# Query, key and value columns summed by feature quarters beside the first conditioning units

## The reference

```python
ada = jax.nn.silu(c) @ lp['w_ada'] + lp['b_ada']
sh1, sc1, g1, sh2, sc2, g2 = [a[:, None, :] for a in jnp.split(ada, 6, axis=-1)]
mix, states = mixer(x * (1 + sc1) + sh1, attend, conv_buf, h0, lp)
x = layer_norm(ALPHA * x + (1 + g1) * mix, lp['ln_g'][0], lp['ln_b'][0])
gt, up = jnp.split((x * (1 + sc2) + sh2) @ lp['w_ffn_in'], 2, axis=-1)
f = (jax.nn.silu(gt) * up) @ lp['w_ffn_out']
x = layer_norm(ALPHA * x + (1 + g2) * f, lp['ln_g'][1], lp['ln_b'][1])
...
proj = h @ lp['w_in'] + lp['b_in']
q, kvc, kvs, kvw, nsa_g, r_x, r_y, merge_g = jnp.split(proj, cuts, axis=-1)
```

## Time and profile before

| | |
|---|---|
| median of three runs | 1774.49 us |
| profiled execution | 1777.09 us, its span 1775.4 us |
| TensorE matmuls busy | 1737.5 us (98%) |
| TensorE weight loads busy | 1602.9 us (90%) |
| VectorE, ScalarE, GpSimd busy | 899.8, 711.3, 157.1 us |
| bytes moved by DMA | 384.05 MB, mean 216 GB/s |
| mean granted clock of TensorE | 0.99 |

### The profile page before, as it was taken

One profiled execution on the slowest core, in us unless ns is written; L12 is line 12 of the kernel. 1 busy time (PEld: TensorE's weight loads), 2 busy tenths in 40 slices (PEclk: granted clock), 3 DMA queues, 4 the chain that ended last, 5 costly groups with the idle time before them and its releaser, 6 DMA issues.

```text
span 1775.4 us, 34441 instructions
## 1 busy us (share of the span) xinstructions
PE 1737.5 (98%) x13514; PEld 1602.9 (90%) x13514; DVE 899.8 (51%) x1632; ACT 711.3 (40%) x1076; POOL 157.1 (9%) x271
## 2 busy tenths in 40 slices
PE   8989999999999999999999999999999999999997
PEld 3558879888999998889988899999999999999997
DVE  3233346655656655565873344444444444444565
ACT  2223227764545443343563333333333333333344
POOL 0001312213322311100000000000000000000001
PEclk9999999999999999999999999999999999999998
DMA  9998878766655647985647855545555454544552
GB/s 362 381 379 302 296 245 299 281 215 237 193 179 176 208 149 277 348 322 173 213 146 258 290 208 165 165 128 163 163 192 182 161 167 159 168 151 138 166 166 80
DMA packets 114151, 384.05 MB, mean 216 GB/s; under 512 B 14941, under 2 KB 15325, under 8 KB 113662
## 3 DMA queue, kind: packets, MB, share of 16 engines
q1 hardware_dynamic: 103248, 349.82, 57.1%
q0 software_dynamic: 10208, 32.32, 5.6%
q10 hardware_dynamic: 590, 0.44, 0.1%
HBM read 373.48 MB, written 9.03 MB: 215 GB/s over the span
## 4 chain that ended last, share of the span: by engine, by line
PE 90%; DMA 5%; DVE 2%; ACT 1%; SPq 1%; issue 1%; POOL 0%; POOLq 0%; ACTq 0%; DVEq 0%
PE bank L714 26%; PE bank L716 25%; PE bank L715 25%; DMA raw<-in_w_units 4%; PE bank L721 3%; PE bank L761 3%; PE bank L739 2%; PE bank L887 1%; SPq L478 1%; DVE wlo L377 1%; PE bank L1007 1%; PE bank L923 1%; DMA mgate<-mg 0%; ACT z L1510 0%; PE bank L954 0%
## 5 line engine op out<-in xcount | busy, mean ns | idle before, releaser
L714 PE MATMUL bank<-xhi,wlo 128*128 128x288 f32 x2544 | 759.2, 298 | 2.3 <-DVE wlo L377 1.7
L715 PE MATMUL bank<-xlo,whi 128*128 128x288 f32 x2544 | 751.0, 295 | 0.0
L716 PE MATMUL bank<-xhi,whi 128*128 128x288 f32 x2544 | 748.7, 294 | 0.0
L377 DVE TENSOR_TENSOR wlo<-raw,whi 128x1024 fp32r<-128x1024 f32 (+2 forms) x468 | 510.2, 1127 | 381.2 <-ACT whi L369 373.9
L369 ACT CAST whi<-raw 128x1024 fp32r<-128x1024 f32 (+2 forms) x468 | 434.6, 969 | 424.2 <-PE bank L716 273.8
L714 PEld LDWEIGHTS bank<-xhi,wlo 128*128 128x128 f32 x2544 | 477.5, 188 | 15.6 <-issue 13.7
L716 PEld LDWEIGHTS bank<-xhi,whi 128*128 128x128 f32 x2544 | 479.6, 189 | 0.0
L715 PEld LDWEIGHTS bank<-xlo,whi 128*128 128x128 f32 x2544 | 478.4, 188 | 0.6
L716 PE MATMUL bank<-hhi,whi 128*128 128x288 f32 x704 | 208.7, 296 | 0.0
L714 PE MATMUL bank<-hhi,wlo 128*128 128x288 f32 x704 | 208.3, 296 | 0.0
L715 PE MATMUL bank<-hlo,whi 128*128 128x288 f32 x704 | 205.2, 292 | 0.0
(11 more groups left out here) (332 smaller groups left out, 1674.9 us busy)
## 6 DMA issues: line engine op xcount, KB each, us to landing
raw<-in_w_units SPq DMA_DIRECT2D x556, 512.0 KB, 6.1
raw<-in_w_ffn_out_units SPq DMA_DIRECT2D x64, 384.0 KB, 3.1
raw<-in_w_ffn_out_units SPq DMA_DIRECT2D x64, 320.0 KB, 3.3
raw<-in_w_units SPq DMA_DIRECT2D x16, 448.0 KB, 8.6
mgate<-mg POOLq DMA_DIRECT2D x32, 144.0 KB, 4.3
mgl<-mgate POOLq DMA_DIRECT2D x16, 288.0 KB, 6.9
bz<-relrow POOLq DMA_DIRECT2D x16, 192.0 KB, 3.6
xt<-in_x SPq DMA_DIRECT2D x8, 288.0 KB, 7.4
```

The costliest lines, as they stand in the source:

```text
L377: nc.vector.tensor_tensor(wlo[e][:, part], raw[:, s, spot], f32(whi[e][:, part]), ALU.subtract).then_inc(raw_used[s][h], 1)
L714: pe.matmul(acc, wt[1][:, w], x[0][:, c, :], start=start, stop=False)
L715: pe.matmul(acc, wt[0][:, w], x[1][:, c, :], start=False, stop=False)
L716: return pe.matmul(acc, wt[0][:, w], x[0][:, c, :], start=False, stop=stop)
```

## The change

INIT becomes 8 A units, three rounds of `"AAG" * 4 + "G"`, and five G units. Its 20 G units are whole units and hold all eight query and all twelve key and value blocks, each by quarters of the features: unit n = 5 kq + r holds feature quarter kq (four chunks) of the four blocks 4r to 4r+3. Round kq multiplies quarter kq, while its eight A units give shift and scale for quarter kq+1. A block's quarter is summed over its four chunks in one bank (a piece, 12 matmuls); the banks go round by seven. VectorE drains each of the 80 pieces: it writes the first quarter with the bias into `qT` or `kvT` and adds the other three to it (`part_out`). QS is gone; KVS is one unit, the gates. The groups G1, SH2 and SC2 are loaded one stage later each: G1 in RNN, SH2 in CMB, SC2 in OUT, whose pattern becomes `"GGAA" * 4 + "GAA" * 4 + "GGGG"`. Their turns and read-outs move with them; SC2 is turned behind OUT's unit 13 and written out in step 14. POOL starts `w1d` and the pages when unit 16 of INIT's 20 is done, two sequences for each unit. The slices of x are loaded ahead of each fourth A unit.

```diff
-INIT = Stage("AAAAG" * 7 + "GAAAA", 1, 0, 0, 0)
-EARLY = 7
-QS = Stage("AAGGAA", 1, INIT.r_end, INIT.g_end, INIT.a_end)
-KVS = Stage("GGAAGGAA", 3, QS.r_end, QS.g_end, QS.a_end)
+LEAD, QUART, BLOCKS, ROUND = 8, 4, 20, 5
+INIT = Stage("A" * LEAD + ("AAG" * 4 + "G") * 3 + "G" * ROUND, 1, 0, 0, 0)
+KVS = Stage("G", 1, INIT.r_end, INIT.g_end, INIT.a_end)
...
-OUT = Stage("GGGG", 4, CMB.r_end, CMB.g_end)
+OUT = Stage("GGAA" * 4 + "GAA" * 4 + "GGGG", 1, CMB.r_end, CMB.g_end, CMB.a_end)
...
         def kv_written(eng):
-            read_out(eng, KVS.g0, KVS.n - 1, 4, 3)
+            eng.wait_ge(part_ok, INIT.g_end * QUART - 2)
+            eng.wait_ge(acc_free[0], INIT.g_end // 2)
+            eng.wait_ge(acc_free[1], INIT.g_end // 2)
...
+        def piece(n, f):
+            m = n * QUART + f
+            return bank[EARLY_BANK[m % 7]][:, 0:T], m
...
-                if pos in INIT.A:
-                    load(INIT, 0, pos, first=pos < RAW_SLOTS)
-                else:
-                    q = pos // 5
+                if pos in INIT.A[3:2 * DC:4]:
+                    q = INIT.A.index(pos) // 4
                     sp.dma_start(xt[:, 2 * q:2 * q + 2, :], a["x"][:, 2 * q:2 * q + 2, :]).then_inc(x_in[q % 2], 16)
-                    load(INIT, 0, pos)
+                load(INIT, 0, pos, first=pos < RAW_SLOTS)
...
-            pool.wait_ge(unit_done, QS.g0 + 2)
+            pool.wait_ge(unit_done, KVS.g0 - 4)
             pool.dma_start(w1d[:], a["cmp_w1"][0]).then_inc(w1_in[0], 16)
             for b in range(DEC_B):
-                pool.wait_ge(unit_done, KVS.g0 + b)
+                pool.wait_ge(unit_done, KVS.g0 - 4 + b // 2)
                 load_pages(0, b)
-            read_out(pool, QS.g0, 0, 2, 0)
+            read_out(pool, KVS.g0, 0, 2, 0)
...
+            def early_unit(n, fs):
+                s, k = INIT.rawG(0, n)
+                kq = n // ROUND
+                whole = n % ROUND == 0
+                for kks in (((0, 1), (2, 3)) if whole else ((0, 1, 2, 3),)):
+                    for f in fs:
+                        acc, m = piece(n, f)
+                        if kks[0] == 0:
+                            pe.wait_ge(raw_used[s][f // 2], k + 1)
+                            if m >= 7:
+                                pe.wait_ge(part_ok, m - 6)
+                        if whole and f == 0:
+                            pe.wait_ge(mod_lo, 2 * kq + kks[0] // 2 + 1)
+                        for kk in kks:
+                            w = slice((f * QUART + kk) * P, (f * QUART + kk + 1) * P)
+                            ins = step(acc, (whi[n % 2], wlo[n % 2]), w, X, kq * QUART + kk, kk == 0, kk == QUART - 1)
+                        if kks[-1] == QUART - 1:
+                            ins.then_inc(*((part_mm, 1) if f < QUART - 1 else (unit_done, 1)))
...
+            pe.wait_ge(ada_out, 1)
+            a_units(INIT, 0, (4, 5, 6, 7))
+            a_turn(1)
+            pe.wait_ge(bias_ok, 1)
+            for n in range(INIT.g_end):
+                kq, r = n // ROUND, n % ROUND
+                if kq == 3 or r == 4:
+                    early_unit(n, range(QUART))
+                    continue
+                u = LEAD + 8 * kq + 2 * r
+                if u % 4 == 0:
+                    pe.wait_ge(ada_out, u // 4)
+                a_units(INIT, 0, (u, u + 1))
+                if r % 2:
+                    early_unit(n, (0, 1))
+                    a_turn(u // 4)
+                    early_unit(n, (2, 3))
+                else:
+                    early_unit(n, range(QUART))
...
-            for j in range(2):
-                plain(QS, 0, j)
-            for u in (2, 3):
-                a_part(QS, 0, u)
-            for i in range(KVS.n):
-                for j in range(4):
-                    plain(KVS, i, j)
-                    a_parts(KVS, i, j)
-            read_out(pe, QS.g0, 0, 2, 0)
+            plain(KVS, 0, 0)
+            kv_written(pe)
+            read_out(pe, KVS.g0, 0, 2, 0)
...
                 if n == 0:
-                    group_turn(SC2)
+                    group_turn(SH2)
                 if n == 8:
                     shift_mean(0)
+                if n == 13:
+                    group_turn(SC2)
+                for u, p in enumerate(OUT.A):
+                    if OUT.G[n] < p < (OUT.G + [OUT.U])[n + 1]:
+                        a_part(OUT, 0, u)
...
+            pe.wait_ge(ada_out, 8 + SC2 + 1)
             norm(0, lambda m: [a_part(FIRST, 0, u) for u in ((0,) if m == 0 else (1, 2))])
...
+            for n in range(INIT.g_end):
+                kq, r = n // ROUND, n % ROUND
+                q = 2 + 2 * kq + r // 2
+                turned = kq < 3 and r in (1, 3)
+                if turned:
+                    a_copy(INIT, 0, q)
+                split_hi(act, *((INIT, 0, n + 1) if n + 1 < INIT.g_end else (KVS, 0, 0)))
+                if turned:
+                    mod_high(0, xm, q, q % 2)
...
+            for n in range(INIT.g_end):
+                kq, r = n // ROUND, n % ROUND
+                q = 2 + 2 * kq + r // 2
+                turned = kq < 3 and r in (1, 3)
+                part_out(n, 0)
+                part_out(n, 1)
+                if turned:
+                    modulated(q)
+                split_lo(dve, *((INIT, 0, n + 1) if n + 1 < INIT.g_end else (KVS, 0, 0)))
+                part_out(n, 2)
+                if turned:
+                    mod_low(0, xm, q, q % 2)
+                part_out(n, 3)
...
                 if c == 1:
+                    group_out(SH2)
+                if c == 14:
                     group_out(SC2)
-                if c == 2:
                     dve.wait_ge(ada_out, 8 + SC2 + 1)
```

More of the change, by code:

```diff
@@ L388, in raw_of @@
             if n < 16:
-                return OUT.raw(n // 4, n % 4)
+                return OUT.rawG(0, n)
             return FIRST.raw(0, n - 16) if n < 20 else NEXT.raw(0, 0)
@@ L472, in load @@
                     rows, size = a["w_units"][r], UNIT
-                if st_ is INIT and pos not in INIT.A:
-                    size = EARLY * 2 * P
                 for h, part, spot in halved(size):
@@ L823, in _ @@
             a_turn(0)
-            for q in range(1, 8):
-                pe.wait_ge(ada_out, q)
-                a_units(INIT, 0, (4 * q, 4 * q + 1))
-                if q == 1:
-                    pe.wait_ge(bias_ok, 1)
-                early_unit(q - 1, (0, 1, 2))
-                a_units(INIT, 0, (4 * q + 2,))
-                early_unit(q - 1, (3, 4))
-                a_units(INIT, 0, (4 * q + 3,))
-                early_unit(q - 1, (5,))
-                a_turn(q)
-            for u in range(2):
-                a_part(QS, 0, u)
-            early_unit(7, range(6))
+            pe.wait_ge(ada_out, 1)
[17 more added lines that the diff above has]
+                    early_unit(n, range(QUART))
             def plain(st_, i, j, ready=None):
@@ L909, in recurrent @@
                     a_parts(RNN, i, j)
-                    if i == 0 and j == 1:
-                        group_turn(G1)
                     if kv is not None and j == 0:
@@ L1020, in _ @@
                 if n == 0:
-                    group_turn(SH2)
+                    group_turn(G1)
                 if n == 1:
-                    pe.wait_ge(ada_out, 8 + SH2 + 1)
+                    pe.wait_ge(ada_out, 8 + G1 + 1)
                 if n in WEIGH:
@@ L1368, in _ @@
                     nc.scalar.activation(zq, zq, ACT.Copy, scale=ALPHA).then_inc(z_pre, 1)
-            group_copy(CMB, SC2)
+            group_copy(CMB, SH2)
             def squares(n, c):
@@ L1418, in _ @@
                     split_hi_n(act, u)
+                if n == 13:
+                    group_copy(OUT, SC2)
                 squares(0, n)
@@ L1597, in _, with modulated @@
             v.tensor_copy(biasCS[:], bank[3][:, 0:NCMP]).then_inc(bias_ok, 1)
-            for q in range(8):
-                if q == 7:
-                    split_lo(dve, INIT, 0, q, EARLY * 2 * P)
+            def modulated(q):
                 a_out(q)
@@ L1605, in _ @@
                 mod_full(0, xt, xm, q, q % 2)
-                if q < 7:
-                    split_lo(dve, INIT, 0, q, EARLY * 2 * P)
-                mod_low(0, xm, q, q % 2)
-                if q == 1:
-                    dve.wait_ge(b_in, SMALL)
-                    v.tensor_scalar(btanh[:], btanh[:], 0.5, None, ALU.mult)
-                    softplus()
-            split_lo(dve, QS, 0, 0)
-            dve.wait_ge(unit_done, INIT.g_end)
-            for u in range(EARLY):
-                ins = v.tensor_scalar(qT[:, u, :], bank[EARLY_BANK[u]][:, 0:T], qb[:, u:u + 1], SCALE, ALU.add, ALU.mult)
-                if u < 2:
-                    ins.then_inc(acc_free[u], INIT.g_end // 2)
@@ new lines, in _ @@
+            for q in range(2):
+                modulated(q)
+                mod_low(0, xm, q, q % 2)
+            split_lo(dve, INIT, 0, 0)
+            dve.wait_ge(b_in, SMALL)
```

(13 more changed lines are left out.)

97 lines of the change are left out of this document (40 added, 57 removed).

## The result

The changed kernel takes 1782.5 us (median of 20 runs, 1775.0 to 1788.1); beside it the kernel before took 1777.3 (20 runs). The ratio is 1.0026, 95% interval 1.0016 to 1.0037: no faster, if anything 5 us slower, where I forecast 10.7 us less. The profiled execution took 1779.0 us (span 1777.3) against 1777.1 before, so it accounts for 1.9 of these 5 us.

A forecast was written before the change was run, and what follows sets the result against it. TensorE, busy 98% of the span, was taken to bound the kernel. 26.3 us gained at compress(0), less 14.9 and 0.7 in OUT, left 10.7: 1777.1 to 1766.4, as a median 1764 us, range 1752 to 1774.

The forecast's parts named there:

- the price of a load: In INIT's rounds and OUT: loading a unit takes 2.64 us, so loads keep within TensorE's time.
- my upper bound: In OUT's dense part: loads cost at most 4 x 1 us of waits; 0 was taken.
- rival (b): In INIT's rounds: landing of loads sets the pace, 23 us lost at 8.0 us landings, time 1787; chance 0.10.
- its own sign: In INIT's rounds: gaps ahead of column units, ended by the subtraction, would show the landing-bound case.
- the 6.1 that it allowed: In INIT's rounds: a half unit must land within about 6.1 us of its issue.
- 201.0: At the end of INIT's rounds and last column units: the gate unit ends at 201.0 us, against 240.1 before.
- The new wait: Ahead of compress(0): TensorE stands 10.5 us for POOL's gates' chain and cmp_pos, plus 1.7 us of lower clock.
- the estimate of 2.15: At the cmp_pos load: 64 KB lands in 2.15 us, compress(0) 3.25 us sooner, time 1760.5; 5.4 was taken.
- The case I named: At the cmp_pos load: the weight queue is full and quiet while TensorE waits; no size of its own.
- the drains stayed hidden: In INIT's rounds: VectorE's drains cost TensorE nothing, 0 taken from bounds 0 and 6 us.
- the term at OUT's end: At OUT's end: writing out SC2 in step 14 costs 0.7 us, bounds 0 and 1.5.
- A pair: In OUT: one conditioning unit takes 0.93 us of TensorE, sixteen 14.9 us.

The follow-up runs named there:

- e4_nosc2: Changed kernel without the sixteen conditioning units of OUT, neither loaded nor multiplied; ratio to the kernel before 0.9877.
- e8_half: Changed kernel loading only half the bytes of each of the rounds' 24 conditioning units, matmuls kept; ratio to the kernel before 0.9982.
- e3_pool: Changed kernel with GpSimd's cmp_pos load and key copies ahead of the gates' chain instead of behind it; ratio to the kernel before 0.9988.
- e15: e14 with the first conditioning unit of each OUT pair also multiplied in the middle of its column unit; ratio to the kernel before 0.9957.
- e14: Changed kernel with e3_pool's and e1's edits, four OUT units moved inside the last merge column units, merge gate then output splits earlier; ratio to before 0.9962.
- e11: Changed kernel with e3_pool's and e1's edits, four OUT units at the merge's end, one conditioning unit per round in mid-column unit; ratio to before 0.9984.
- e2: Changed kernel with OUT's sixteen conditioning units spread evenly over its first twelve column units; ratio to the kernel before 1.0020.
- e1: Changed kernel with ScalarE's copy of SC2 ahead of the splits of units 15 and 16 in OUT's step 13; ratio to the kernel before 1.0024.

## Why the prediction was wrong

**The step that failed** is the price of a load, 2.64 us for a unit, in both places where I set loading against TensorE's time.

In OUT: "3 units in 8.3 us against 3 x 2.64 = 7.9 us of loading ... Bounds 0 and 4 x 1 us, I take 0, since a column unit's slot comes free one unit ahead." It measured 9.7 us (25.98 less 16.3; 9.3 against e4_nosc2, which has the second turn too), more than twice my upper bound. The size was wrong, and the bound with it. The 2.64 us per unit (397 GB/s) came from 21 to 24 us, where TensorE takes each half as it lands. In OUT's dense part the DMA engines are busy 0.97 and move 346 GB/s, so three units take 9.1 us, and TensorE asks for them every 8.4 (6.40 and 2.04). The slot that "comes free one unit ahead" gives a cover, but a lasting deficit uses up any cover. The bound then left out what hangs on a late split: the copy for the second turn behind it (2.84 us) and the lower clock behind each wait (2.8 us), which I had counted at `compress(0)` and not here.

In the rounds: "Its loads are 13 x 2.64 + 2 x 1.49 = 37.3 us, so TensorE is the limit there, by 4.5 us." The rounds ask for 13 units and 1.18 MB of x in 41.8 us, 354 GB/s; 322 were moved from 40 to 160 us. This is rival (b), by its own sign: gaps ahead of column units ended by the subtraction, and halves that land in 7.2 us, above the 6.1 that it allowed. e8_half shows the cause. The gates' unit ended at 208.1 in place of 201.0, a third of the 23 us that I gave (b): 5.4 us of waits for splits past 40 us and 1.3 us of lower clock (0.24 us per matmul from 38.3 to 41.2 us). That is the best of twelve profiles. In the middle one the sigmoid is 13 us late, which is more than OUT lost, and in the latest 16. It goes some way to explain why the median is 3.5 us above the profiled run; the other executions left no trace.

**The new wait** was right in place and cause, but half as long as forecast: 5.2 us in place of 10.5. From the gates' sigmoid to the issue of `cmp_pos` it took 11.2 us in place of 13.5, and the landing 2.38 in place of 5.4; the clock cost 1.57, as forecast (1.7). That `compress(0)` starts at 222.44 + 1.57 = 224.0, only 1.8 us off the forecast 222.2, is luck: rounds 7 us too late and a wait 5.3 us too short nearly cancel. e3_pool gives 6.7 us back, so this wait was on the path to the end.

The landing of 2.38 us is near the estimate of 2.15 from the Trainium skill (DMA: Bandwidth & Descriptors, section Anatomy of one DMA), which I set aside for the rows of before; in five other profiles with this order it is 2.05 to 2.21. In e3_pool, where weights are in the queue at that time, it is 4.3 to 4.8. The case I named, a quiet queue, was there (DMA share 0.12 from the issue to the landing), and the fixed part plus rate holds in it.

**Right**: first column unit at 38.33 (forecast 38.5; its own terms add up to 38.3); the drains stayed hidden (0.45 to 0.51 us each, and no wait named them); the term at OUT's end was 0 (VectorE stands idle for 2.18 us ahead of the last unit, as it did for 1.90). A pair costs 2.04 us, not 1.86: sixteen units 16.3 in place of 14.9.

In sum I had 26.3 - 14.9 - 0.7 = 10.7 us gained. The profile has 24.5 at `compress(0)`, 24.1 at OUT, less 26.0: 1.9 lost. Of the 12.6 us between, 11.1 are OUT; in most of the twelve profiles the rounds add to that.

**Where the lead goes without the give-backs.** It should be 24.5 + 6.7 - 16.3, some 15 us. e15's profiled execution is 12.5 us ahead of the kernel before (span 1762.9 against 1775.4): its sigmoid is at 208.18, as early as the changed kernel's, and OUT holds 2.3 us more than six pairs (111.5 against 96.98 + 6 x 2.04), which leaves 12.6. e14's is 6.0 us ahead (span 1769.4): its sigmoid is at 215.59, 7.4 us later, and OUT holds 1.2, which leaves 6.3. So the rounds take the rest, and how much differs from one execution to the next; by their ratios e14 and e15 gain some 7 us.

**Open.** Whether the four slots or the transfers' rate sets the rounds' waits was not separated: e8 halves both, and e11, which frees the two slots of one pair in each round apart, still waits 11.8 us. What makes the gates' sigmoid 9 us later in one execution than in another was not tested either.

## What to carry to other kernels

Take the rate of loading from a stretch where the buffers are in steady use, at the pattern's own density, and compare demand with it in GB/s, stage by stage. Here the rate read where TensorE waited for every load (397 GB/s) was not reached where column units had to be fed too (322 over the rounds, 346 in OUT's dense part). In OUT, where demand was above what was moved, prefetch depth and order only shifted the waits (three edits, no gain); with four units fewer, the copy first and 293 GB/s OUT had no wait left. When work leaves a stage, list what its length was hiding on other queues: here a chain of small DMAs, mended by two lines. And take more than one profile of a kernel whose loads are tight: behind the same rounds the gates' sigmoid started at 208 us in one execution and at 217 in another.

## What the runs showed of the hardware

The lower clock behind a wait, in three rows: TensorE came back at 852.17 with matmuls every 0.13 us, went to 0.24 some 1.4 us later and stayed there for 3.4 us; behind the turn at 877.99, and behind the 2.58 us wait of e2, the matmuls were slow from the first one on, for 2.9 and 3.3 us. So the waits of 2.74 and 2.84 us cost over 4 each. It can be longer: behind e1's wait for the token sums the granted clock was 0.50 for 10.2 us, from 890.8 to 901.0. Two conditioning units between column units cost 0.19 us beyond their matmuls, alike in each of three repeats at 776.65, 791.50 and 806.34. The same 64 KB load issued by GpSimd landed in 2.05 to 2.38 us beside a quiet weight queue and in 4.3 to 6.2 beside a busy one.
